# The state-space scan: squares of the gated outputs on ScalarE, their sum a turn later on VectorE, the ones product behind the turn's other products

## What is computed

```
y = (y_f + y_b) + xs * d_skip                    # both scan directions, 32 heads of 64
y = y.reshape(bsz, t, SSM_D_INNER) * silu(z)     # SSM_D_INNER = 2048
yg = y.reshape(bsz, t, SSM_GROUPS, SSM_D_INNER // SSM_GROUPS)      # 8 groups of 256
yg = yg * lax.rsqrt(jnp.mean(jnp.square(yg), -1, keepdims=True) + RMS_EPS)
y = yg.reshape(bsz, t, SSM_D_INNER) * norm_w
return y @ w_out                                 # 2048 x 1024
```

## Time and profile before

| | |
|---|---|
| median of 3 runs | 2378.24 us (2377.7 to 2378.41) |
| the profiled execution | 2379.42 us |
| its span | 2377.5 us |
| mean granted TensorE clock | 0.993 |
| busy: TensorE matmul, VectorE, ScalarE, GpSimd | 98%, 41%, 18%, 3% |
| chain that ended last: TensorE, VectorE, DMA | 93%, 3%, 3% |
| the scan's turns 2 to 15 | 493 to 579 us |
| TensorE idle before VectorE's L117 in the whole span | 13.9 us in 10 waits |

### The profile page before, as it was taken

The page is one execution under the profiler, slowest core; times in us unless marked ns, Lnnn a source line. Parts: engine busy times, 40 slices in busy tenths (PEclk is TensorE's granted clock), DMA queues, the critical chain, the costliest instruction groups (busy, mean ns, idle before and its releaser), DMA issues.

```text
span 2377.5 us, 24384 instructions
## 1 busy us (share of the span) xinstructions
PE 2333.4 (98%) x10310; PEld 1388.3 (58%) x10310; DVE 970.1 (41%) x1839; ACT 430.5 (18%) x971; POOL 75.3 (3%) x130
## 2 busy tenths in 40 slices
PE   8999999999999999999899999999999999999998
PEld 5568548875586448786444444435878644444443
DVE  3567656677576544462222221222355321122112
ACT  3310003365100021220111111111122021111111
POOL 2000000010100000000000000000000000000000
PEclk9999999999999999999999999999999999999999
DMA  7379625354796342256899999993325589999995
GB/s 283 127 308 394 234 89 190 131 202 165 283 406 258 129 160 102 93 216 244 338 427 428 427 428 428 426 411 123 138 92 228 229 359 427 427 428 428 428 426 238
DMA packets 57434, 671.53 MB, mean 282 GB/s; under 512 B 7312, under 2 KB 7600, under 8 KB 18528
## 3 DMA queue, kind: packets, MB, share of 16 engines
q1 hardware_dynamic: 50160, 649.45, 67.1%
q0 software_dynamic: 7152, 20.39, 2.5%
HBM read 666.56 MB, written 3.26 MB: 282 GB/s over the span
## 4 chain that ended last, share of the span: by engine, by line
PE 93%; DVE 3%; DMA 3%; ACT 0%; issue 0%; POOL 0%; SPq 0%; DVEq 0%; POOLq 0%; ACTq 0%
PE ps L101 91%; DMA ring<-in_mlp_w 1%; DVE arena L117 1%; DVE arena L114 1%; DMA arena<-ssm_rows 1%; PE ps L323 1%; PE ps L2465 1%; DMA ring<-in_attn_w_in 1%; PE ps L2447 0%; PE ps L593 0%; DVE X L117 0%; PE ps L1722 0%; DVE arena L110 0%; ACT arena L106 0%; PE ps L1184 0%
## 5 line engine op out<-in xcount | busy, mean ns | idle before, releaser
L101 PE MATMUL ps<-arena 128*64 128x512 f32 (+5 forms) x3656 | 864.2, 462 | 5.8 <-DVE arena L117 3.7
L101 PEld LDWEIGHTS ps<-arena 128*128 128x128 f32 (+2 forms) x3656 | 418.0, 168 | 370.0 <-issue 351.8
L101 PE MATMUL ps<-XTGB,ring 128*128 128x256 f32 x2544 | 565.7, 381 | 5.0 <-DMA ring<-in_mlp_w 5.0
L101 PE MATMUL ps<-ring,arena 128*64 128x512 f32 (+1 forms) x1808 | 555.0, 593 | 0.0
L101 PEld LDWEIGHTS ps<-XTGB,ring 128*128 128x128 f32 x2544 | 479.9, 190 | 78.9 <-issue 7.8
L101 PEld LDWEIGHTS ps<-ring,arena 128*64 128x64 f32 (+1 forms) x1808 | 195.7, 149 | 284.9 <-issue 282.5
L117 DVE TENSOR_TENSOR arena<-ps,arena 128x512 f32<-128x512 f32 (+4 forms) x166 | 96.0, 613 | 364.8 <-PE ps L101 351.4
L101 PE MATMUL ps<-ring,XTGB 128*128 128x512 f32 (+3 forms) x568 | 226.6, 557 | 1.6 <-DMA ring<-in_attn_w_in 1.0
L101 PE MATMUL ps<-XTGB,arena 128*64 128x512 f32 (+1 forms) x576 | 197.6, 499 | 0.0
L121 ACT COPY arena<-ps 128x512 f32<-128x512 f32 (+2 forms) x169 | 75.7, 469 | 601.1 <-PE ps L101 279.5
L117 DVE TENSOR_TENSOR arena<-arena,ps 128x512 f32<-128x512 f32 x36 | 24.8, 688 | 388.6 <-PE ps L101 388.6
(11 more groups left out here) (140 smaller groups left out, 924.0 us busy)
## 6 DMA issues: line engine op xcount, KB each, us to landing
ring<-in_exp_w SPq DMA_DIRECT2D x88, 2048.0 KB, 19.6
arena<-in_exp_w SPq DMA_DIRECT2D x80, 2048.0 KB, 18.7
ring<-in_mlp_w SPq DMA_DIRECT2D x26, 2048.0 KB, 8.9
XTGB<-in_exp_w SPq DMA_DIRECT2D x20, 2048.0 KB, 19.4
ring<-in_ada_w SPq DMA_DIRECT2D x19, 2048.0 KB, 10.1
ring<-in_ssm_w_in SPq DMA_DIRECT2D x12, 2048.0 KB, 7.8
ring<-in_w_in SPq DMA_DIRECT2D x12, 2048.0 KB, 7.8
ring<-in_gate_w SPq DMA_DIRECT2D x12, 2048.0 KB, 7.8
```

Of the source, the lines that this page charges most:

```text
L101: return self.e.matmul(o, lhsT=lhsT, rhs=rhs, start=start, stop=stop, skip_group_check=True)
```

## The change

norm_a on VectorE keeps only the product with the gate. ScalarE makes the squares in the same odd turn, behind exps, z_out and z_silu (`squares(g)`). VectorE adds the two tiles in the next, even turn, behind least and in front of cb_group (`norm_sum(g)`). On TensorE the ones product of that even turn stands behind z_chunk or so_part and no longer in front of them.

```
@@ ssm_pe
                 if 2 <= i < SP + 2:
                     apply(i - 2)
-                if i >= 4 and i % 2 == 0 and (i - 4) // 2 < 8:
-                    norm_b((i - 4) // 2)
                 if i < 12:
                     z_chunk(pe, 4 + i)
                 elif i < 16:
...
                 elif i < 19:
                     for q in range(2):
                         so_part(pe, 1 + (i - 16) // 2, 2 * (i % 2) + q)
+                if i >= 4 and i % 2 == 0 and (i - 4) // 2 < 8:
+                    norm_b((i - 4) // 2)
 
             for s, q in ((3, 0), (3, 1), (2, 2), (2, 3), (3, 2)):
                 so_part(pe, s, q)
@@ ssm_act
+            def squares(g):
+                act.wait_ge(at("yz", g))
+                act.then_inc(act.act(xcT[:, 2 * g:2 * g + 2, :], zT[:, 2 * g:2 * g + 2, :], ACT.Square), ("yz2", g))
+
...
                     k = z_out(4 + i)
                     if i % 4 == 3:
                         z_silu(1 + i // 4, k)
+                if i >= 3 and i % 2 == 1 and (i - 3) // 2 < 8:
+                    squares((i - 3) // 2)
@@ ssm_dve
             def norm_a(g):
                 z2, x2 = zT[:, 2 * g:2 * g + 2, :], xcT[:, 2 * g:2 * g + 2, :]
                 v.wait_ge(at("y", 2 * g), at("y", 2 * g + 1), at("z silu", g // 2))
-                k = v.then_inc(v.tt(z2, x2, z2, ALU.mult))
-                v.wait_ge(k)
-                k = v.then_inc(v.tt(x2, z2, z2, ALU.mult))
-                v.wait_ge(k)
-                v.then_inc(v.tt(x2[:, 0, :], x2[:, 0, :], x2[:, 1, :], ALU.add), ("ysq", g))
+                v.then_inc(v.tt(z2, x2, z2, ALU.mult), ("yz", g))
+
+            def norm_sum(g):
+                v.wait_ge(at("yz2", g))
+                v.then_inc(v.tt(xcT[:, 2 * g, :], xcT[:, 2 * g, :], xcT[:, 2 * g + 1, :], ALU.add), ("ysq", g))
...
                 if i < SP:
                     least(i)
-                    if i % 2 == 0:
-                        cb_group(i // 2)
+                if i >= 4 and i % 2 == 0 and (i - 4) // 2 < 8:
+                    norm_sum((i - 4) // 2)
+                if i < SP and i % 2 == 0:
+                    cb_group(i // 2)
                 if 1 <= i <= SP:
                     weigh(i - 1)
```

## The result

The change takes 2381.91 us (median of 20 runs, 2378.82 to 2387.07); the kernel before takes 2378.91 us in the 20 runs beside it. The ratio is 1.0013, 95% interval 1.0007 to 1.0019: 3.0 us longer (1.7 to 4.5), clear of no change, but under the 0.2%, 4.8 us, from which the prediction counts a difference. The profiled execution of the change has 2381.68 us and a span of 2379.8, against 2379.42 and 2377.5.

What follows compares the result with a forecast made beforehand. The prediction took a four-turn ring of fetch, VectorE and TensorE, late by 1.5 us a round, to bound the scan. Scan -2.15, last group +3.46 and clock +1.66 gave +3.0 us, 2381.2 us, range 2378.3 to 2384.2.

Steps and rivals of the forecast that it cites:

- What bounds the scan: Scan: TensorE idle in every second two-turn stretch, three in all, so an order can give at most some 4.4 us.
- the ring through fetch, VectorE and TensorE: Scan, four turns a round: row fetch, VectorE's weights, TensorE's apply; 24.8 us against 23.2 of matmuls, late by 1.5.
- The square leaves VectorE: VectorE in front of weigh(5): 0.72 us less a round, three rounds, 2.15 us gained.
- The square arrives on ScalarE: ScalarE's odd turns: Square takes 0.63 us, no table load; sum waits behind the Silu, 0.6 us covered by slack.
- TensorE's order: Ones product behind z_chunk: TensorE waits once, at apply(5); without this move the first gain would be lost only in part.
- The last group: Scan's end: norm_b(7) directly in front of so_part(3,0) leaves Ln, Exp and scaling exposed, TensorE idle 3.46 us.
- The clock: Behind the last group's idle time TensorE's clock falls to 1.2 GHz, adding 1.66 us, bounds 0 and 3.3.
- The sum: Whole kernel: -2.15 +3.46 +1.66 gives +3.0 us, 2381.2 us.
- Rival A: Scan gives nothing or costs, as the sum waits on VectorE's queue: 2383.4 to 2385.1 us, chance 0.16.
- Rival B: Clock behind the last group isn't lowered, or only while TensorE is idle: +1.3 us, 2379.5, chance 0.17.
- C: All idle time of the scan goes, as the fetch starts earlier: +0.7 us, 2378.9, chance 0.05.
- D: norm_b(7)'s move isn't exposed, something shorter releases so_part(3,0): -2.15 us, 2376.1, chance 0.02.

Runs made afterwards that it cites:

- e4: Kernel before with only TensorE's order changed, squares and sum left on VectorE: 2385.35 us, +6.4 us against before.
- e9: The change, group 7's ones product between slab 2's parts, square ahead of z_out, norm_c of groups 0 to 5 behind weigh: 2374.40 us, -4.4 against before.
- e5: The change with TensorE's order as before, ones product in front of z_chunk: 2380.83 us, +1.9 us against before.
- e1: The change itself, timed again beside the kernel before: 2380.68 us, +1.7 us against before.
- e8: The change with each Square made twice in a row on ScalarE: 2382.55 us, +3.7 us against before.
- e2: The change with group 7's ones product between so_part(2,0) and so_part(2,1): 2376.48 us, -2.5 us against before.
- e6: The change with the square ahead of z_out and z_silu in ScalarE's odd turns: 2380.05 us, +1.2 us against before.

## Why the prediction was right, point by point

**What bounds the scan** was right: the ring through fetch, VectorE and TensorE, late three times. e4 and e9 show it from both sides. The bound of 4.4 us on what an order can give was 0.5 too low: the view counts TensorE as busy for 69.52 us of the stretch before and for 69.03 in e9, so short waits lay hidden in the busy time.

**The square leaves VectorE**: the mechanism was right, the size somewhat too small. 2.15 us were forecast, 3.3 are seen against the one profile of before, and 2.55 of these are VectorE's. Its part of the round shrank by 0.85 us and not 0.72. In norm_a each link started 0.02 us after the end of the one that it waited for; in the change the product and the sum have other work behind them, which starts 0.08 us before their recorded ends (516.30 + 0.69 against 516.91, 518.75 + 0.41 against 519.09). The remaining 0.7 us are the slow fetches of that profile (e4). All late fetches together run from 6.2 to 6.8 us with no order that I can name, so I count this as scatter.

**The square arrives on ScalarE**: 0.63 us in the trace, as estimated (not the 2.1 that the prediction set beside it and left out), and no table load beside it (8 instructions more on ScalarE, the eight squares). The idle time behind the Silu, forecast as 0.6 us and covered by the round's slack, is 0.33 to 0.45. That cover is used up, though: this road has become the round's length, which the prediction didn't see, since it still counted the fetch as the bound.

**TensorE's order**: that the first gain is lost only in part without it was wrong (e5). The step had TensorE wait twice, as before, and left out that the sum now ends 1.0 us later behind the arrival of the rows than norm_a did. With the ones product in front, apply(5) stands behind that sum, and the 0.70 us that it waited before is less than the 1.0.

**The last group**: right. 3.46 us forecast, 3.30 idle, and 3.54 us longer from apply(15) to the transposition where the clock stayed (e1). The two pieces of ada work and the weight load cost nothing, as forecast: the adding of rows still had 4.20 us idle before it, and 1.38 in e1, where the clock did not stretch the matmuls. Of the drain that the Trainium skill counts with a table load ("ScalarE: Activation LUTs", "What ACT_TABLE_LOAD costs") the trace after again shows none: 599.88 plus 1.28 is 601.16, and Exp starts at 601.18.

**The clock**: its fall was forecast at 1.66 us. The profiled execution has 2.8, the others of this idle time 0, 1.7 and 3.0, and the mean is near 1.8. The direction and the mean stand. The argument for it doesn't: it took 3.46 us to cost since a single idle time of 1.96 had, while the profiles have idle times of 2.00 to 2.46 us that cost nothing, and in e1 one of 3.30.

**The sum**: -2.15 +3.46 +1.66 = +3.0 was forecast and +3.0 measured (+1.7 and +2.1 in the later series). From the measured terms it is -2.55 +3.54 +1.8 = +2.8. So the order of the terms is no luck, but the match to the tenth is: the scan's gain was taken 0.4 us too small and the other two together 0.2 too small, and the repetitions lie 1 us lower. Rival A fell: the sum never waits in the late half, where it starts 1.1 us after the square's end, and e8 bears that out. Rival B is what e1's profile shows; as a statement on every execution it is wrong. C's total idle time gone needed two further moves (e9). D fell too: so_part(3,0) waits for the scaling (3.30 <-DVE arena L114).

## What to carry to other kernels

When a step is moved behind "the turn's other work", look at the last turn by itself: a latency that every other turn hides is bare where the loop ends, and one exception for it (e2) can turn a loss into a gain. In a ring over several engines, find all roads of nearly the same length before counting a gain; here removing the road through the Silu showed the one through the fetch, 0.1 us shorter (e6), and only both together reached TensorE's own work (e9). And two edits which each give nothing alone (e4, e5) can gain together, so an edit is not refuted by its half.

## What was not expected of the hardware

After the same idle time of 3.30 us the granted clock of TensorE fell in five of six profiled executions and not in the sixth, and where it fell, the 40 matmuls behind took 19.1 us (three times), 20.2 or 20.4 instead of 17.4. So one profile doesn't give the price of an idle time of this length: it is 0, 1.7 or about 3 us. Shorter ones are no surer: behind waits for weights of 1.89 to 2.46 us the clock fell in some executions and not in others, with no order by length.
